# Two layers on one core: first expert's weights loaded beside the routing, a small sine network moved beside another layer's product, unused output tiles zeroed early

## The chip, the core and the metric

The kernel runs on one core of a Trainium2 chip. A core has five engines with a program each: TensorE (PE, matrix products), VectorE (DVE), ScalarE (ACT), GpSimd (POOL) and SyncE (SP), which here mostly issues DMA transfers. They share an on-chip memory of 128 partitions (SBUF), an accumulator memory (PSUM) and 16 DMA engines. The metric is the device time of one execution in microseconds (us), lower is better.

## The reference, cut to what matters

The program is two layers over 1024 rows of 1024 fp32 numbers. The first is a mixer (two recurrences), an output product with a residual and a norm, and a mixture of 32 experts of which each row takes two:

```python
def hier_moe(h, wg, bg, we, be, w_gate, w_up, w_down):
    """Top-1 expert group, then top-2 experts within it; gate = p(group) * softmax(top-2 logits)."""
    ...
    ids = (g_sel * EXPERTS_PER_GROUP + top_i).reshape(-1).astype(jnp.int32)
    order = jnp.argsort(ids)
    tok = order // TOP_K
    xs = xf[tok]
    sizes = jnp.bincount(ids, length=N_EXPERTS).astype(jnp.int32)
    hg = lax.ragged_dot(xs, w_gate.astype(xs.dtype), sizes)
    hu = lax.ragged_dot(xs, w_up.astype(xs.dtype), sizes)
    ys = lax.ragged_dot(jax.nn.silu(hg) * hu, w_down.astype(xs.dtype), sizes)
    ...
```

The second layer has a long convolution whose filters come from positions alone, by a small network of sines. It depends on weights and a table of positions, and on nothing that the first layer computes:

```python
    h = jnp.sin(sf[0] * (feats @ fw1.astype(f32) + fb1.astype(f32)))
    h = jnp.sin(sf[1] * (h @ fw2.astype(f32) + fb2.astype(f32)))
    h = jnp.sin(sf[2] * (h @ fw3.astype(f32) + fb3.astype(f32)))
    h = (h @ fw4.astype(f32)).reshape(L, HY_ORDER, 2, HY_WIDTH)
```

With this kernel's inputs (drawn from a fixed seed) the routing gives each of the 32 experts between 29 and 112 rows, counted with the reference's router on the host. So every expert fills one tile of 128 rows and none fills two.

## The kernel before, in words

The order of the work is written out by hand: the program is a sequence of stages (`Stage`), each with one instruction list per engine, semaphores between them, and a barrier of all five engines at its end (L118). What an engine does in a stage starts only when all engines have ended the stage before. Every fp32 operand of a large product is split in two: a rounded part "hi", which ACT copies, and the rest "lo", which DVE subtracts from the original. A product is then three matmuls (`products3`, L156 to L158).

The stages that the change touches, in the order in which they run, with P = 128 rows a tile:

- **g1** (`gemm`, 58 to 640 us) is the first layer's input product. While it runs, POOL sets 47 tiles of the DRAM array `xs` to zero from one zero row block in SBUF (`clear`, L401 to L407): the sorted rows of the experts are written into it later, and unused places must be zero.
- **go** (`deep_norm`, L3639, 948.4 to 1189.9 us) is the output product: 4 passes over 2 row tiles, 16 units of the contraction each, 64 units in all. A unit loads a 128x1024 block of weights (SP), ACT makes its hi (L3813), DVE its lo (L3882) and the lo of 256 columns of activations (L3887), TensorE does 12 matmuls. Weights and halves have three buffers. From the second pass on DVE and ACT also do residual and norm of the pass before.
- **route** (L1374, 1190 to 1258 us) picks the experts, counts, sorts, and leaves in `tile_exp` for each of 47 tiles the expert that it belongs to, and the number of tiles used (`n_used`). SP loads constants and the rows `h2t`; POOL scatters rows to `xs`.
- **moe** (`experts`, L1528 to L1731, 1258.9 to 1903.4 us) loops over the 47 tiles. For a tile SP loads its 128 rows of `xs` and three weight matrices of 2 MB, each in two halves of 1 MB (`weights`, L1572 to L1575), from the expert named in `tile_exp`; each load of a half waits until the lo of the tile before has been taken from that place. A DMA with a false condition (`cond`) moves nothing and counts its semaphore all the same. For the 15 tiles behind the last used one ACT runs `skipped` (L1693 to L1695): it stores whatever is in the buffer `y`, so that the DRAM array `ys` is written everywhere.
- **hf** (`hyena_spectrum`, L2012, 2434.1 to 2654 us) starts with the sine network: SP issues 18 small loads (L2053 to L2060), then the 1.8 MB table of transform matrices (L2061), the 1 MB `w4` in two halves (L2063), `skip` and the window (L2065). TensorE, DVE and ACT run the three layers of the network in a chain (L2104 to L2113, L2151 to L2166, L2133 to L2135), then TensorE multiplies with `w4` (`filters`) and DVE multiplies with the window (L2176). The table's lo is POOL's (L2148).
- **hc** (`hyena`, L2197) is the convolution itself. POOL makes the lo of its two tables, `ft_lo` and `it_lo` (L2347 to L2352).

## Time and profile before

| what | us |
|---|---|
| median of 3 runs | 4482.77 (4481.86 to 4484.9) |
| the profiled execution | 4481.31 |
| its span (first to last instruction) | 4479.5 |
| stage g1 | 58 to 640 |
| stage go | 948.4 to 1189.9 |
| stage route | 1190 to 1258 |
| stage moe | 1258.9 to 1903.4 |
| stage hf | 2434.1 to 2654 |

Over the span TensorE is busy for 3660.7 us (82%), DVE for 2936.8 us (66%), ACT for 1695.2 us (38%) and POOL for 66.7 us (1%). Since each stage ends in a barrier, the end of the program moves by what each stage gains or loses, and each stage has to be read for itself. A row of the timeline gives the start, the duration, the engine, the line and the operation with its shapes; in brackets stands how long the engine had been idle and what released it. SPq and ACTq are the DMA queues that SP and ACT issue to; their time is that of issuing, and the landing comes later.

### The profile page before, as it was taken

Reading aid. Unit: us, or ns where it says so; the run is one execution under the profiler, and the core shown is the slowest. Engines: PE = TensorE matmul, PEld = TensorE weight load, DVE = VectorE, ACT = ScalarE, POOL = GpSimd, SP = SyncE. Lnnn points to the kernel's source line nnn. Section 1 sums busy time; section 2 is a strip of 40 time slices with the busy share of each in tenths; the row PEclk is TensorE's granted clock in tenths of the full one; section 3 lists DMA queues with packets and bytes.
Section 4 is the critical chain, followed back from the end, with each engine's and each line's share of the span. In section 5 each row is a group of like instructions: output and inputs, shape, how many; then the busy total and the mean of one; then the engine's idle time right before and its main releaser. Section 6 shows DMA issues by size and latency. Waiting matters only on the chain. (4 is left out here: it accounts for less than half of the span.)

```text
span 4479.5 us, 63351 instructions
## 1 busy us (share of the span) xinstructions
PE 3660.7 (82%) x25152; PEld 2997.1 (67%) x25152; DVE 2936.8 (66%) x3525; ACT 1695.2 (38%) x2202; POOL 66.7 (1%) x49
## 2 busy tenths in 40 slices
PE   6999966879769999739997454546999786999898
PEld 4888856768657777628885243316998465888786
DVE  4774327966458888778874779884555546666455
ACT  3222113545257777633332132262333224323244
POOL 0000000000010000010000000000000000000000
PEclk8999988989779999859998576778999798999999
DMA  6523216646399999753332032263110332222465
GB/s 232 196 85 108 86 52 190 198 148 193 128 365 399 398 398 398 284 184 103 105 122 103 21 123 71 90 155 97 41 41 24 131 122 76 85 85 85 157 194 166
DMA packets 355480, 698.57 MB, mean 156 GB/s; under 512 B 55400, under 2 KB 159864, under 8 KB 353050
## 3 DMA queue, kind: packets, MB, share of 16 engines
q1 hardware_dynamic: 321754, 578.34, 37.8%
q10 hardware_dynamic: 22688, 74.98, 4.4%
q0 software_dynamic: 10784, 41.70, 2.4%
q8 instruction: 180, 2.95, 0.3%
q14 instruction: 74, 0.61, 0.0%
HBM read 535.88 MB, written 170.60 MB: 158 GB/s over the span
## 5 line engine op out<-in xcount | busy, mean ns | idle before, releaser
L1709 DVE TENSOR_TENSOR moe_wg_lo<-moe_wg,moe_wg_hi 128x2048 fp32r<-128x2048 f32 x68 | 155.6, 2291 | 69.5 <-ACT moe_wg_hi L1663 69.5
L156 PE MATMUL g_ps<-h1T_hi,g_w_lo 128*128 128x512 f32 x448 | 175.2, 391 | 7.0 <-DVE g_w_lo L339 7.0
L157 PE MATMUL g_ps<-h1T_lo,g_w_hi 128*128 128x512 f32 x448 | 175.0, 391 | 0.0
L158 PE MATMUL g_ps<-h1T_hi,g_w_hi 128*128 128x512 f32 x448 | 174.9, 390 | 0.0
L1663 ACT ACTIVATE moe_wg_hi<-moe_wg 128x2048 fp32r<-128x2048 f32 x68 | 130.2, 1918 | 95.0 <-DMA moe_wg<-in_exp_w_gate 95.0
L156 PE MATMUL g_ps<-x2T_hi,g_w_lo 128*128 128x512 f32 x352 | 140.0, 398 | 24.3 <-DVE g_w_lo L558 24.3
L3882 DVE TENSOR_TENSOR x3T_lo<-fd_w_raw,x3T_hi 128x1024 fp32r<-128x1024 f32 x66 | 80.8, 1224 | 120.1 <-ACT x3T_hi L3813 119.9
L2793 PE MATMUL rs_p_p<-rs_pm,rs_qx 64*64 64x64 f32 x2048 | 157.6, 217 | 0.0
L156 PE MATMUL fd_acc<-x3T_hi,x3T_lo 128*128 128x512 f32 x352 | 139.7, 397 | 18.3 <-DVE x3T_lo L3885 18.3
L1709 DVE TENSOR_TENSOR moe_wu_lo<-moe_wu,moe_wu_hi 128x2048 fp32r<-128x2048 f32 x68 | 152.5, 2282 | 1.8 <-ACT moe_wu_hi L1663 1.8
L156 PE MATMUL g_ps<-g_w_hi,h1T_lo 128*128 128x512 f32 x384 | 149.4, 389 | 0.0
L157 PE MATMUL g_ps<-g_w_lo,h1T_hi 128*128 128x512 f32 x384 | 149.4, 389 | 0.0
L158 PE MATMUL g_ps<-g_w_hi,h1T_hi 128*128 128x512 f32 x384 | 149.4, 389 | 0.0
L1709 DVE TENSOR_TENSOR moe_wd_lo<-moe_wd,moe_wd_hi 128x2048 fp32r<-128x2048 f32 x66 | 147.9, 2281 | 0.0
L2793 PEld LDWEIGHTS rs_p_p<-rs_pm,rs_qx 64*64 64x64 f32 x2048 | 143.8, 134 | 0.1
L157 PE MATMUL g_ps<-x2T_lo,g_w_hi 128*128 128x512 f32 x352 | 140.0, 398 | 0.0
L158 PE MATMUL g_ps<-x2T_hi,g_w_hi 128*128 128x512 f32 x352 | 139.5, 396 | 0.0
L1663 ACT ACTIVATE moe_wu_hi<-moe_wu 128x2048 fp32r<-128x2048 f32 x68 | 129.7, 1912 | 25.2 <-DMA moe_wu<-in_exp_w_up 25.2
L157 PE MATMUL fd_acc<-x3T_lo,x3T_hi 128*128 128x512 f32 x352 | 139.1, 395 | 0.0
L158 PE MATMUL fd_acc<-x3T_hi 128*128 128x512 f32 x352 | 138.9, 395 | 0.0
L1663 ACT ACTIVATE moe_wd_hi<-moe_wd 128x2048 fp32r<-128x2048 f32 x66 | 126.5, 1920 | 24.4 <-DMA moe_wd<-in_exp_w_down 24.3
L383 DVE COPY g_st<-g_ps 128x512 f32<-128x512 f32 x24 | 16.6, 691 | 177.5 <-PE g_ps L158 177.5
(702 smaller groups left out, 11000.3 us busy)
## 6 DMA issues: line engine op xcount, KB each, us to landing
moe_wg<-in_exp_w_gate SPq DMA_DIRECT2D x68, 1024.0 KB
moe_wu<-in_exp_w_up SPq DMA_DIRECT2D x68, 1024.0 KB
moe_wd<-in_exp_w_down SPq DMA_DIRECT2D x66, 1024.0 KB
fd_w_raw<-in_ffn_w_down SPq DMA_DIRECT2D x66, 512.0 KB, 4.4
go_w_raw<-in_w_out SPq DMA_DIRECT2D x64, 512.0 KB
...
s_xs<-g_zero POOLq DMA_DIRECT2D x1, 24064.0 KB, 82.8
...
```

Of the source, the lines that this page charges most:

```text
L156: pe.matmul(out, l[1], r[0], start=(k == 0), stop=False)
L157: pe.matmul(out, l[0], r[1], start=False, stop=False)
L158: return pe.matmul(out, l[0], r[0], start=False, stop=(k == kt - 1))
L383: v.tensor_copy(st[:, j % 2, 2 * i + 1], ps[:, 2 * i + 1]).then_inc(by_dve, 1)
L1663: act.activation(hi[:, q * m:q * m + m], w[:, q * m:q * m + m], ACT.Copy).then_inc(sem_hi, 1)
L1709: v.tensor_tensor(lo[:, q * m:q * m + m], w[:, q * m:q * m + m], hi[:, q * m:q * m + m], ALU.subtract).then_inc(sem_lo, 1)
L2793: mm = pe.matmul(p_p[g][o, p], q, pm[o, k], start=True, stop=True)
L3882: v.tensor_tensor(w_lo[:, n % NB], w_raw[:, n % NR], w_hi[:, n % NB], ALU.subtract).then_inc(w_low, 1)
```

## The change

**The experts' weights.** The three fp32 weight buffers now belong to the caller and live through route and moe. In route SP loads expert 0's gate, up and down weights (3 x 2 MB) right behind `h2t` and waits for them at its end. `tile_exp` has 48 more columns: for each tile whether its expert differs from that of the tile before (for the first tile: from expert 0), times `n_used`. In moe a weight load is made only if that value is over the tile's number; SP reads two more values a step for it.

**Unused tiles.** In g1 POOL clears, behind the 47 tiles of `xs`, also the last 31 tiles of `ys` (16.25 MB). In moe the 15 stores of `skipped` become a `nop` that counts the same semaphore.

**The sine network** is now a class `FilterNet` that runs as an `aside` in go, and stores its 128x512 result to DRAM (`net`); hf loads it with one transfer.

**POOL's subtractions** in hf (`tb_lo`) and hc (`ft_lo`, `it_lo`) are DVE's now. In hf the table's load stands behind those of h, w4 and skip.

```diff
@@ gemm
-                pool.dma_start(rows(clear)[:, 0:N_TILE], bc(zero[:, :].unsqueeze(1), [P, N_TILE, D])).then_inc(zeroed, 16)
-                pool.wait_ge(zeroed, 16)
+                for to in clear:
+                    n = to.shape[0] // P
+                    pool.dma_start(rows(to), bc(zero[:, :].unsqueeze(1), [P, n, D])).then_inc(zeroed, 16)
+                pool.wait_ge(zeroed, 16 * len(clear))
@@ route
             sp.dma_start(h2t[:, :, :], rows(h2)).then_inc(h_in, 16)
+            for dst, src in first:
+                sp.dma_start(dst[:, :, :], rows(src)).then_inc(w_in, 16)
+            sp.wait_ge(w_in, past(16 * len(first)))
...
+            v.tensor_scalar(te[:, N_LIST + 1:N_LIST + 2], te[:, 0:1], 0.0, None, ALU.not_equal)
+            v.tensor_tensor(te[:, N_LIST + 2:], te[:, 1:N_LIST], te[:, 0:N_LIST - 1], ALU.not_equal)
+            v.tensor_copy(tile_exp[:, N_LIST:N_LIST + 1], te[:, N_LIST:N_LIST + 1])
+            v.drain()
+            v.tensor_scalar(tile_exp[:, N_LIST + 1:], te[:, N_LIST + 1:], te[:, N_LIST:N_LIST + 1], None, ALU.mult)
@@ experts
+            def fresh(j):
+                return sp.value_load(tile_exp[0:1, bass.ds(j + (N_LIST + 1), 1)], min_val=0, max_val=N_TILE)
...
-            def weights(sem, w, src, e, j, n_used, q):
+            def weights(sem, w, src, e, j, limit, q):
                 n = w.shape[1] // 2
                 sp.dma_start(w[:, q * n:q * n + n], src.rearrange("e (q k p) n -> e q p k n", p=P, q=2)[e, q],
-                             cond=(n_used > j)).then_inc(sem[q], 16)
+                             cond=(limit > j)).then_inc(sem[q], 16)
...
             def skipped(j, b):
-                act.dma_start(ys.rearrange("(j p) n -> j p n", p=P)[j - 1], y[:, 1 - b]).then_inc(stored[1 - b], 16)
+                act.nop().then_inc(stored[1 - b], 16)
@@ hyena_spectrum
-            sp.dma_start(ft[:, :], feats_t).then_inc(got, 16)
-            sp.dma_start(wa[:, :], w1).then_inc(got, 16)
...
-            sp.dma_start(raw, table).then_inc(table_in, 16)
+            sp.dma_start(h[:, :], net).then_inc(got, 16)
             for r in half:
                 sp.dma_start(w4_raw[r], w4.rearrange("p (o d n) -> p o d n", o=2, d=2)).then_inc(got4, 16)
             sp.dma_start(sk[:, :, :], skip.rearrange("(a o) n -> a o n", a=1)).then_inc(got4, 16)
+            sp.dma_start(raw, table).then_inc(table_in, 16)
...
+            v.wait_ge(got4, past(48))
+            v.tensor_tensor(wp[:, :, 0], w4_raw[:, :, 0], w4_raw[:, :, 1], ALU.add)
+            v.tensor_tensor(wp[:, :, 1], w4_raw[:, :, 0], w4_raw[:, :, 1], ALU.subtract).then_inc(summed, 1)
+            v.wait_ge(tab_high, past(1))
+            v.tensor_tensor(tb_lo[:, :, :], raw, tb_hi[:, :, :], ALU.subtract).then_inc(tab_low, 1)
@@ hyena
-        @block.gpsimd
-        def _(pool):
-            pool.wait_ge(ft_high, past(1))
-            pool.tensor_tensor(ft_lo[:, :, :], raw, ft_hi[:, :, :], ALU.subtract).then_inc(ft_low, 1)
-            pool.wait_ge(it_high, past(1))
-            pool.tensor_tensor(it_lo[:, :, :], i_raw, it_hi[:, :, :], ALU.subtract).then_inc(it_low, 1)
...
+            v.wait_ge(ft_high, past(1))
+            v.tensor_tensor(ft_lo[:, :, :], raw, ft_hi[:, :, :], ALU.subtract).then_inc(ft_low, 1)
...
                     if i:
                         rest(i - 1)
+                    if c == 0 and i == 1:
+                        v.wait_ge(it_high, past(1))
+                        v.tensor_tensor(it_lo[:, :, :], i_raw, it_hi[:, :, :], ALU.subtract).then_inc(it_low, 1)
+class FilterNet:
...
+    def multiply(self, pe, q):
+        if q == 0:
+            pe.wait_ge(self.got, past(18 * 16))
+        else:
+            pe.wait_ge(self.sine, past(q))
+        for c, r in enumerate(self.HALF):
+            if q:
+                w = (self.wb, self.wc)[q - 1]
+                mm = pe.matmul(self.ps[r, :], w[r, :], self.h[r, :], start=True, stop=True)
+            else:
+                mm = pe.matmul(self.ps[r, :], self.wa[:, :], self.ft[:, c * 512:c * 512 + 512], start=True, stop=True)
+        mm.then_inc(self.product, 1)
+
+    def reduce(self, v, q):
+        k, m = self.k, self.m
+        v.wait_ge(self.got, past(18 * 16))
+        v.wait_ge(self.product, past(q + 1))
...
+    def activate(self, act, q):
+        act.wait_ge(self.arg, past(q + 1))
+        act.activation(self.h[:, :], self.m[:, :], ACT.Sin).then_inc(self.sine, 1)
+
+    def store(self, sp):
+        sp.wait_ge(self.sine, past(3))
+        sp.dma_start(self.out, self.h[:, :]).then_inc(self.kept, 16)
@@ deep_norm
+        ASIDE, AHEAD = (5, 15, 25), 4
...
+                if aside is not None and n == 2:
+                    aside.load(sp)
+                if aside is not None and n == ASIDE[2] + 3 * AHEAD:
+                    aside.store(sp)
...
+                if aside is not None and n in ASIDE:
+                    aside.multiply(pe, ASIDE.index(n))
...
                 split(n)
+                if aside is not None and n - AHEAD - 1 in ASIDE:
+                    aside.activate(act, ASIDE.index(n - AHEAD - 1))
...
                 split(n)
+                if aside is not None and n - AHEAD in ASIDE:
+                    aside.reduce(v, ASIDE.index(n - AHEAD))
```

So TensorE does a layer of the network behind units 5, 15 and 25 of go, DVE its eight instructions behind its part of units 9, 19 and 29, and ACT the sine behind its part of units 10, 20 and 30.

VectorE's instructions in the second pass of go, around units 19 and 20, before; `go_w_lo` and `go_a_lo` are the lo parts of a unit's weights and activations:

```order
L3882 TENSOR_TENSOR go_w_lo<-go_w_raw,go_w_hi 128x1024
L3887 SCALAR_TENSOR_TENSOR go_a_lo<-mixT,go_fac,go_a_hi 128x256
L3882 TENSOR_TENSOR go_w_lo<-go_w_raw,go_w_hi 128x1024
L3887 SCALAR_TENSOR_TENSOR go_a_lo<-mixT,go_fac,go_a_hi 128x256
L3905 TENSOR_SCALAR go_var<-go_ssq 128x1 x2
L3882 TENSOR_TENSOR go_w_lo<-go_w_raw,go_w_hi 128x1024
L3887 SCALAR_TENSOR_TENSOR go_a_lo<-mixT,go_fac,go_a_hi 128x256
```

And after, at the same place:

```order
L3943 TENSOR_TENSOR go_w_lo<-go_w_raw,go_w_hi 128x1024
L3948 SCALAR_TENSOR_TENSOR go_a_lo<-mixT,go_fac,go_a_hi 128x256
L3659 TENSOR_SCALAR go_net_m<-go_net_ps,go_net_bb,go_net_sf 128x512
L3661 TENSOR_SCALAR go_net_k<-go_net_m 128x512
L3663 TENSOR_SCALAR go_net_k<-go_net_k 128x512
L3665 TENSOR_SCALAR go_net_k<-go_net_k 128x512
L3668 SCALAR_TENSOR_TENSOR go_net_m<-go_net_k,go_net_m 128x512 x3
L3670 TENSOR_SCALAR go_net_m<-go_net_m 128x512
L3943 TENSOR_TENSOR go_w_lo<-go_w_raw,go_w_hi 128x1024
L3948 SCALAR_TENSOR_TENSOR go_a_lo<-mixT,go_fac,go_a_hi 128x256
L3966 TENSOR_SCALAR go_var<-go_ssq 128x1 x2
```

The network's eight instructions (`go_net_m`, `go_net_k`) now stand in a row between unit 19's and unit 20's subtractions.

VectorE at the head of hf before, from the first layer of the network on; `hf_wp` is the sum and the difference of w4's halves:

```order
L2155 TENSOR_SCALAR hf_m<-hf_p_f,hf_bb,hf_sf 128x512
L2157 TENSOR_SCALAR hf_k<-hf_m 128x512
L2159 TENSOR_SCALAR hf_k<-hf_k 128x512
L2161 TENSOR_SCALAR hf_k<-hf_k 128x512
L2164 SCALAR_TENSOR_TENSOR hf_m<-hf_k,hf_m 128x512 x3
L2166 TENSOR_SCALAR hf_m<-hf_m 128x512
L2169 TENSOR_TENSOR hf_wp<-hf_f 128x2x512
L2170 TENSOR_TENSOR hf_wp<-hf_f 128x2x512
L2155 TENSOR_SCALAR hf_m<-hf_p_f,hf_bb,hf_sf 128x512
```

And after:

```order
L2133 TENSOR_TENSOR hf_wp<-hf_f 128x2x512
L2134 TENSOR_TENSOR hf_wp<-hf_f 128x2x512
L2136 TENSOR_TENSOR hf_tb_lo<-hf_w,hf_tb_hi 128x3456
L2142 TENSOR_TENSOR hf_f<-hf_p_f,hf_win 128x1024 x4
L2146 TENSOR_TENSOR hf_f<-hf_f,hf_sk 1x512
```

The network is gone, the table's subtraction stands behind `hf_wp` and ahead of the four window products.

SyncE's loads at the head of go before:

```order
L3695 DMA go_fac<-in_mix_norm 128x16
L3721 DMA go_w_raw<-in_w_out 128x1024 x3
L3724 DMA go_wr<-in_norm_w 128x1024
L3721 DMA go_w_raw<-in_w_out 128x1024
L3701 DMA go_r<-in_x 128x1024
L3721 DMA go_w_raw<-in_w_out 128x1024
```

And after:

```order
L3746 DMA go_fac<-in_mix_norm 128x16
L3772 DMA go_w_raw<-in_w_out 128x1024 x3
L3775 DMA go_wr<-in_norm_w 128x1024
L3632 DMA go_net_ft<-in_c_feats 33x1024
L3633 DMA go_net_wa<-in_hy_filt_w_2 33x64
L3636 DMA go_net_wb<-in_hy_filt_w_2 64x64
L3636 DMA go_net_wc<-in_hy_filt_w_2 64x64
L3638 DMA go_net_bb<-in_hy_filt_b_2 64x1
L3639 DMA go_net_sf<-in_hy_sin_freq 64x1
```

The network's loads (18, of which the first six are shown) stand behind the first three weight blocks and the norm's weights, and ahead of unit 3's block.

## Rows read from the trace of the kernel before

**Rows 1.** Busy time by stretch (start:end, length): PE, PEld, DVE, ACT, POOL, clock, DMA share, GB/s.

```profile
100.00:120.00 20.00, 20.00 (x90) 16.58 (x89) 14.98 (x14) 3.52 (x5) 0.00 (x0) 1.00 1.03 417
1030.00:1060.00 30.00, 28.69 (x157) 24.44 (x156) 15.68 (x20) 13.60 (x18) 0.00 (x0) 0.97 0.56 181
1190.00:1260.00 70.00, 18.98 (x88) 18.85 (x88) 16.85 (x99) 1.61 (x3) 15.36 (x16) 0.50 0.46 182
1400.00:1500.00 100.00, 97.56 (x458) 79.63 (x457) 89.23 (x56) 74.62 (x55) 0.00 (x0) 1.00 1.04 398
2434.00:2460.00 26.00, 3.25 (x8) 0.58 (x8) 5.88 (x9) 5.00 (x3) 3.19 (x1) 0.50 0.59 179
```

**Rows 2.** Transfers by destination and source (part 6): count, KB each, us to landing.

```profile
moe_wd<-in_exp_w_down SPq DMA_DIRECT2D x66, 1024.0 KB
s_xs<-g_zero POOLq DMA_DIRECT2D x1, 24064.0 KB, 82.8
```

**Rows 3.** Timeline, start of the expert stage: start, us, engine, line, operation, [idle<-releaser].

```profile
1260.05 0.97 SPq L1574 DMA_DIRECT2D moe_wg<-in_exp_w_gate  x2
1267.27 1.91 ACT L1663 ACTIVATE moe_wg_hi<-moe_wg 128x2048 fp32r<-128x2048 f32 x1 [1.87 <-DMA moe_wg<-in_exp_w_gate]
1269.21 2.29 DVE L1709 TENSOR_TENSOR moe_wg_lo<-moe_wg,moe_wg_hi 128x2048 fp32r<-128x2048 f32 x1 [2.55 <-ACT moe_wg_hi L1663]
```

**Rows 4.** Timeline, end of the expert stage, ScalarE's and SyncE's queues.

```profile
1881.10 17.07 ACTq L1695 DMA_DIRECT2D s_ys<-moe_y  x15
1903.42 2.20 SPq L1779 DMA_DIRECT2D nf_hw<-in_hy_conv_w  x3
```

**Rows 5.** Tile moe_y after 1880 us: durations ns min/median/max, and its landings.

```profile
L1695 ACTq DMA_DIRECT2D s_ys<-moe_y x15: 343/657/1194, 1881.1 to 1897.2; - x15
DMA to landing us min/median/max: 2.7/5.6/5.9
```

**Rows 6.** Timeline, head of the spectrum stage hf, in order of time.

```profile
2434.06 0.37 SPq L2053 DMA_DIRECT2D hf_ft<-in_c_feats  x1
2445.02 0.59 SPq L2061 DMA_DIRECT2D hf_w<-in_c_hft  x1
2446.71 1.97 PE L2112 MATMUL hf_p_f<-hf_ft,hf_wa 33*64 33x512 f32 x4 [18.93 <-DMA hf_sf<-in_hy_sin_freq]
2453.64 3.08 ACT L2132 ACTIVATE hf_tb_hi<-hf_w 128x3456 fp32r<-128x3456 f32 x1 [24.05 <-DMA hf_w<-in_c_hft]
2456.74 1.28 ACT L2135 ACT_TABLE_LOAD   x1
2456.81 7.46 POOL L2148 TENSOR_TENSOR hf_tb_lo<-hf_w,hf_tb_hi 128x3456 fp32r<-128x3456 f32 x1 [515.93 <-ACT hf_tb_hi L2132]
2458.72 6.63 DVE L2169 TENSOR_TENSOR hf_wp<-hf_f 128x1024 f32<-128x1024 f32 x1 [4.43 <-DMA hf_sk<-in_hy_skip]
2466.41 0.80 DVE L2155 TENSOR_SCALAR hf_m<-hf_p_f,hf_bb,hf_sf 128x512 f32<-128x512 f32 x1
2471.09 0.43 DVE L2166 TENSOR_SCALAR hf_m<-hf_m 128x512 f32<-128x512 f32 x1
2492.52 1.22 DVE L2176 TENSOR_TENSOR hf_f<-hf_p_f,hf_win 128x1024 f32<-128x1024 f32 x1 [2.19 <-PE hf_p_f L2084]
```

**Rows 7.** Timeline, the output product go in its first pass.

```profile
983.82 1.23 DVE L3882 TENSOR_TENSOR go_w_lo<-go_w_raw,go_w_hi 128x1024 fp32r<-128x1024 f32 x1 [1.10 <-ACT go_w_hi L3813]
986.54 1.23 DVE L3882 TENSOR_TENSOR go_w_lo<-go_w_raw,go_w_hi 128x1024 fp32r<-128x1024 f32 x1 [1.10 <-ACT go_w_hi L3813]
993.60 1.06 ACT L3813 ACTIVATE go_w_hi<-go_w_raw 128x1024 fp32r<-128x1024 f32 x1 [1.26 <-PE go_acc L158]
```

**Rows 8.** Timeline, the convolution stage hc.

```profile
2678.85 4.48 DVE L1924 TENSOR_TENSOR hc_w<-shT 128x2048 f32<-128x2048 f32 x2
2720.09 6.70 DVE L2397 TENSOR_TENSOR hc_w<-hc_w 128x512 f32<-128x512 f32 x1
2726.29 0.79 PE L156 MATMUL hc_ps<-hc_hi,hc_it_lo 128*128 128x512 f32 x1 [11.03 <-POOL hc_it_lo L2352]
```

More of the change, by code:

```diff
@@ L2132, in _ @@
             act.activation(tb_hi[:, :, :], raw, ACT.Copy).then_inc(tab_high, 1)
-            for q in range(3):
-                act.wait_ge(arg, past(q + 1))
-                act.activation(h[:, :], m[:, :], ACT.Sin).then_inc(sine, 1)
             for n in range(5):
@@ L3737, in _ @@
                 store(t)
-            for b in range(n_r):
-                sp.wait_ge(stored[b], past(16 * len(range(b, NT, n_r))))
+            for b in range(n_out):
+                sp.wait_ge(stored[b], past(16 * len(range(b, NT, n_out))))
+            if aside is not None:
+                aside.finish(sp)
         @block.gpsimd
```

177 lines of the change are left out of this document (91 added, 86 removed).

## The prediction

> **What bounds the kernel now.** I looked for the stages that the change touches and read each by itself, since a barrier ends each and only a stage's own last chain counts.
>
> First the busy time by stretch [rows 1]. In the middle of the expert stage the 16 DMA engines are busy all the time (share 1.04, 398 GB/s) while DVE, the busiest other engine that prepares weights, works 89.23 of 100 us: that stage is bound by transfers. In the output product go (1030 to 1060) TensorE is busy 28.69 of 30 us at a granted clock of 0.97: bound by TensorE. In g1 (100 to 120) TensorE is busy 20.00 of 20 us although the zeroing of `xs` drives the DMA to 417 GB/s. In route (1190 to 1260) the DMA share is 0.46.
>
> Then the transfers [rows 2]: a half of a weight matrix is 1.049 MB (1024 KB), and 66 such loads of `wd` are 33 steps of two, 32 used tiles and one that loads nothing. A used tile moves 6 x 1.049 + 0.52 (rows in) + 0.52 (rows out) = 7.34 MB, 18.4 us at 398 GB/s; DVE's work would let it go in 0.892 x 18.4 = 16.4 us.
>
> Then the timeline where stages begin and end: the start of the expert stage [rows 3], its end [rows 4, 5], the head of hf [rows 6], the units of go [rows 7] and the places in hc where POOL was waited for [rows 8].
>
> **A, start of the expert stage: -7 us (bounds -2 to -10).** Of all weight loads in the stage only expert 0's six halves go, since the 32 tiles have 32 different experts; "none twice in a row" finds nothing to skip. The six halves are 6.29 MB, 15.8 us at the stage's rate. But the stream of loads now starts later. Before, the first half was issued at 1260.05 [rows 3] into idle queues. After, the first load of weights is tile 1's gate, which must wait until tile 0's first half has been split. ACT was free at 1267.27 - 1.87 = 1265.40 (it then has x's hi behind it), copies 1.91 us, DVE subtracts 2.29 us: the first issue is at 1269.6, so 9.6 us later. In that gap x of tile 1 passes (1.3 us that the stream saves), and I give back 0.5 us for smaller gaps behind it, since the next halves follow at DVE's pace of 2.29 us while one takes 1.049/0.398 = 2.63 us on the DMA. -15.8 + 9.6 - 1.3 + 0.5 = -7.0. At best two of the remaining latencies overlap more (-10); at worst the cold start of 7.2 us (1260.05 to 1267.27) comes again in full behind the first load and little but 2 us is left. The 6.29 MB need 16 us in route, whose DMA share is 0.46 over 70 us [rows 1] and whose h2t is ahead of them in the queue; they end some 35 us before the stage does. Route itself gets three small DVE instructions and a drain: +0.5 us. SP's two further reads a step stand ahead of loads that have some 10 us of queued transfers before them: 0.
>
> The Trainium skill ("DMA: Bandwidth & Descriptors", section "Anatomy of one DMA — SWDGE (gpsimd) path") gives a transfer a fixed cost of about 2 us beside its bytes at about 436 GB/s, which is 4.4 us for 1 MB. The row shows 7.2 us for the cold start here, on another kind of queue, and the row decides; by the page the stream would be restarted sooner and A would be an estimated -9.
>
> **B, end of the expert stage: -15 us (-12 to -17).** The 15 stores of unused tiles hold ACT's queue for 17.07 us from 1881.10 [rows 4], the last lands 5.6 us (median) after issue [rows 5], and the next stage's first instruction is at 1903.42. The issues take 15 x 0.657 = 9.9 us, so each turn of the loop costs another (17.07 - 9.9)/14 = 0.5 us. After, 15 turns with a nop: 1880.8 + 15 x 0.5 = 1888.4. What is late next lies below it: the last real store, issued just before 1881, lands by 1886, and DVE's last subtraction ends at about 1884. Gain 1903.4 - 1888.4 = 15. A turn may cost 0.35 to 0.7 us, hence the bounds. The 16.25 MB are now written in g1, behind `xs`. There TensorE stayed at 20.00 of 20 under 417 GB/s [rows 1], `xs` took 82.8 us for 24 MB [rows 2], so `ys` ends some 56 us later, near 200, in a stage that ends at 640: 0. If its cover were gone it would cost up to its 56 us.
>
> **C, head of hf: -29 us (-27 to -34).** Before: 18 issues of 0.6 us from 2434.06 to 2445.02, then the table, which lands 8.6 us later at 2453.64; ACT's copy of it (3.08 us) stands ahead of the first sine, then come two more layers, and the fourth window product ends at 2492.52 + 1.22 = 2493.7 [rows 6]. After: the table is issued behind h, w4 and skip, at about 2436. The queue had both behind one another before: w4 and skip landed at 2458.72, 5.1 us after the table. So the sum of both is what the table now waits: 2434.06 + 0.3 + 8.6 + 5.1 + 0.6 (h, 0.26 MB) = 2448.6. ACT's copy to 2451.7. DVE now does the table's lo: 2.29 us for 2048 columns [rows 3] is 1.12 ns a column, 3456 columns are 3.87 us, to 2455.6. DVE did `hf_wp` before that, and the two PSUM buffers of the first window products are full. Two window products (1.22 each), then TensorE's third and fourth group at 3.41 us each (2.19 + 1.22 between windows), and the last window: 2455.6 + 1.2 + 3.4 + 3.4 + 1.2 = 2464.8. Gain 2493.7 - 2464.8 = 28.9. If the table lands without the 5.1 us, up to 5 us more; if h's transfer adds its own latency, 2 us less. DVE's `hf_wp` of 6.63 us shrinks, since POOL worked beside it (its 7.46 us instruction spans it), but it is off the last chain.
>
> **D, the network in go: +8 us (+4 to +16).** TensorE sets the end here and a unit takes 986.54 - 983.82 = 2.72 us [rows 7]. Per layer TensorE does two fp32 products, 1.97 us in hf [rows 6] at a clock of 0.50 [rows 1] and about 1.0 at 0.97. DVE gets a block of 2471.09 + 0.43 - 2466.41 = 5.1 us between two units' subtractions. It idles 1.10 us in each unit [rows 7], and its lo is up to one unit (2.7 us) ahead of TensorE thanks to three buffers: 5.1 - 1.1 - 2.7 = 1.3, with the smaller idle time in the passes that also do the norm 1.5 us of stall. Three times 1.0 + 1.5 is 7.5, and 0.5 for ACT, which does a table load of 1.28 us for the sine, another back to its root, and the sine of 0.63, and which idles 1.26 us a unit [rows 7]. If DVE's lead covers it all: 3 x 1.0 + 1 = 4. If ACT's six table loads all show: 7.5 + 6 x 1.28 = 15.2, say 16. SP's 18 issues (11 us) fall ahead of unit 3's load, where three units are in flight; up to 1.6 us late at the start of the stage, in the range.
>
> **E, hc: 0 (-3 to +4).** `ft_lo` (3200 columns x 1.12 = 3.6 us) goes ahead of DVE's first work at 2678.85. `it_lo` costs another 3.6 and about 1.5 of waiting, but a product of 6.70 us at 2720.09, beside POOL, becomes as short as others of 128x512 (0.80 us at 2466.41 [rows 6]), and TensorE, which waited 11.03 us for POOL's `it_lo` until 2726.29, is released some 3.4 us sooner [rows 8]: +3.6 - 3.4.
>
> **The sum.** -7 + 0.5 - 15 - 29 + 8 + 0 = -42.5, against the profiled execution of 4481.3: 4438.8. The median of the runs is 1.5 us above the profiled one: 4440.
>
> **Rivals.**
>
> *The network is dear in go.* If the table loads and the DVE block both show, D is +16 to +20 and the time some 4450. For: ACT's table load of 1.28 us is in the row, and with a norm in the same pass each sine costs two. Against: at 2456.74 the load is followed by the sine at once (2458.04), and ACT has slack. The Trainium skill ("ScalarE: Activation LUTs", section "What ACT_TABLE_LOAD costs") gives a switch about 2.66 us with its drain, twice the row; six of them would be 16 us and D at most an estimated +16 to +20 too. Chance 12%.
>
> *The start of the expert stage is worth something else.* All 15.8 us if the stream finds its pace at once (4431), or 2 us if a full cold start comes again (4445). Each for half of 6%.
>
> *The routing repeats experts*, so that the rule of the change bites: each repeat would drop up to 6.29 MB, but not below DVE's 16.4 us for 18.4: 2 us for most tiles, more where buffers run ahead; for all 31 it would be 62 us, about 4380. Against: the 32 experts have one tile each. 3%. This is also the case in which the change does more than its loads suggest; in the forecast that part does nothing.
>
> *Slower: TensorE's clock falls in go.* Each aside makes TensorE wait; if the granted clock falls to 1.2 GHz, a unit's matmuls (28.69/30 of 2.72 = 2.6 us at 0.97) take 2.6 x 0.97/0.50 = 5.05 us, so +2.3 a unit. Eighteen units at that clock eat the whole gain, and all of the 54 units behind the first aside would give +125 and 4565. Against: the clock was 0.97 there with DVE's and ACT's waits of 1.3 us in each unit. For: at the head of hf, where TensorE is busy 3.25 of 26 us, and in route it was 0.50 [rows 1]. 4%.
>
> **How the numbers follow.** The forecast has 75%: 4440. The range takes in the bounds of A to E that do not all fall to one side and the first two rivals: 4426 to 4458. A difference under 0.2% (9 us) can hardly be told from none in this kernel. The forecast, the third rival and most of the first two are faster by over 9 us: 0.94; the far end of the first is within 0.2%: 0.02; the last is slower: 0.04.
>
> **What the changed profile would show.** Route ends no later than before but for 0.5 us, and the first tile's hi starts at once. The first gate load of moe is issued near 9 us after the stage's start and the stage is 22 us shorter. ACT's nops end 7 to 8 us after the last real store. hf's fourth window product ends 31 us after its start instead of 60. go is 8 us longer, with three waits of TensorE near units 9, 19, 29, each of 1 to 2 us. It is wrong if go grows by over 16 us or its clock falls, if tiles in moe take another time than 18.4 us, or if g1 ends later.

## The result, and the profile after

The changed kernel takes 4439.24 us (median of 4 runs, 4436.19 to 4441.13) against 4483.36 us of the kernel before measured beside it (4 runs, 4481.86 to 4484.9): a ratio of 0.9898, 95% interval 0.9885 to 0.991. The forecast was 4440. The profiled execution took 4440.7 us, its span is 4438.9.

Since every stage ends in a barrier, the two traces can be set against each other stage by stage. This table is worked out from the times at which SyncE leaves the barriers. The stages that no edit touches differ here by -1.2 to +0.7 us, and by up to 2.8 us in single stages of the kernels further down, which is how far one profiled execution can be trusted.

| stage | before, us | after - before | forecast |
|---|---|---|---|
| g1 | 586.1 | +0.1 | 0 |
| go | 241.7 | +9.6 | +8 |
| route | 68.0 | +0.4 | +0.5 |
| moe | 645.3 | -20.9 | -22 |
| hf | 220.3 | -30.5 | -29 |
| hc | 243.2 | -0.1 | 0 |
| all | 4479.5 | -40.6 | -42.5 |

Start of moe, timeline of the changed kernel, all engines; it answers to [rows 3]:

```profile
1268.68 0.34 SPq L1611 DMA_DIRECT2D moe_x<-s_xs  x1
1274.79 3.70 ACT L1676 ACTIVATE moe_wg_hi<-exp_g 128x2048 fp32r<-128x2048 f32 x2
1276.72 4.49 DVE L1722 TENSOR_TENSOR moe_wg_lo<-exp_g,moe_wg_hi 128x2048 fp32r<-128x2048 f32 x2 [0.57 <-ACT moe_wg_hi L1676]
1279.33 2.53 SPq L1587 DMA_DIRECT2D exp_g<-in_exp_w_gate  x2
```

The stage begins at 1267.8. ACT splits gate weights at 1274.79 without a wait, and SyncE's first load that moves weights (tile 1's) is issued at 1279.33, once VectorE has taken the first half: 11.5 us after the stage's start, against 2.0 before. The forecast was 9.6 us of delay, and it is 9.5.

End of moe, and the tile moe_y behind 1880 us; they answer to [rows 4, 5]:

```profile
1883.02 4.49 DVE L1722 TENSOR_TENSOR moe_wd_lo<-exp_d,moe_wd_hi 128x2048 fp32r<-128x2048 f32 x2
1883.21 0.34 ACTq L1704 DMA_DIRECT2D s_ys<-moe_y  x1
1892.31 2.26 SPq L1792 DMA_DIRECT2D nf_hw<-in_hy_conv_w  x3
DMA to landing us min/median/max: 2.6/2.6/2.6
```

From the last real store to the next stage it is 9.1 us instead of 23.4. Busy time by stretch, columns as in [rows 1]:

```profile
160.00:200.00 40.00, 40.00 (x178) 33.12 (x177) 27.41 (x26) 9.65 (x12) 0.00 (x0) 1.00 0.96 380
1400.00:1500.00 100.00, 98.85 (x464) 81.23 (x463) 89.45 (x57) 76.14 (x55) 0.00 (x0) 1.00 1.04 399
```

The zeroing of ys runs in g1 at 160 to 200 (380 GB/s, 106 in the kernel before), and TensorE is busy for 40.00 of 40 us. In the middle of moe nothing has changed: 399 GB/s, DMA share 1.04.

Head of hf, timeline; it answers to [rows 6]:

```profile
2423.25 0.34 SPq L2058 DMA_DIRECT2D hf_h<-s_net  x1
2425.35 0.37 SPq L2062 DMA_DIRECT2D hf_w<-in_c_hft  x1
2431.85 1.23 DVE L2133 TENSOR_TENSOR hf_wp<-hf_f 128x1024 f32<-128x1024 f32 x1 [14.16 <-DMA hf_sk<-in_hy_skip]
2435.97 3.08 ACT L2120 ACTIVATE hf_tb_hi<-hf_w 128x3456 fp32r<-128x3456 f32 x1 [17.19 <-DMA hf_w<-in_c_hft]
2439.09 3.76 DVE L2136 TENSOR_TENSOR hf_tb_lo<-hf_w,hf_tb_hi 128x3456 fp32r<-128x3456 f32 x1 [4.88 <-ACT hf_tb_hi L2120]
2442.76 2.35 DVE L2142 TENSOR_TENSOR hf_f<-hf_p_f,hf_win 128x1024 f32<-128x1024 f32 x2
2451.26 1.22 DVE L2142 TENSOR_TENSOR hf_f<-hf_p_f,hf_win 128x1024 f32<-128x1024 f32 x1 [2.19 <-PE hf_p_f L2082]
```

The table lands 12.7 us after the stage's start and the fourth window product ends at 2452.48, 29.2 us after it, instead of 59.7.

The first layer of the network in go, VectorE, ScalarE and one wait of TensorE; it answers to [rows 7]:

```profile
986.23 1.23 DVE L3943 TENSOR_TENSOR go_w_lo<-go_w_raw,go_w_hi 128x1024 fp32r<-128x1024 f32 x1 [1.17 <-ACT go_w_hi L3872]
987.77 0.80 DVE L3659 TENSOR_SCALAR go_net_m<-go_net_ps,go_net_bb,go_net_sf 128x512 f32<-128x512 f32 x1
989.34 1.28 ACT L3675 ACT_TABLE_LOAD   x1
992.47 0.43 DVE L3670 TENSOR_SCALAR go_net_m<-go_net_m 128x512 f32<-128x512 f32 x1
992.93 0.63 ACT L3675 ACTIVATE go_net_h<-go_net_m 128x512 f32<-128x512 f32 x1 [2.31 <-DVE go_net_m L3670]
993.04 1.23 DVE L3943 TENSOR_TENSOR go_w_lo<-go_w_raw,go_w_hi 128x1024 fp32r<-128x1024 f32 x1
994.81 0.47 PE L156 MATMUL go_acc<-go_w_hi,go_a_lo 128*128 128x512 f32 x1 [1.55 <-DVE go_a_lo L3948]
997.82 1.06 ACT L3872 ACTIVATE go_w_hi<-go_w_raw 128x1024 fp32r<-128x1024 f32 x1 [1.57 <-PE go_acc L158]
```

The network's eight instructions stand from 987.77 to 992.9, unit 10's subtraction comes behind them without idle time, and TensorE waits 1.55 us for VectorE (994.81). ACT's next copies run on until TensorE is the one waited for again (997.82).

hc, VectorE's timeline and TensorE's waits (us in total, times, longest); it answers to [rows 8]:

```profile
2637.21 3.48 DVE L2320 TENSOR_TENSOR hc_ft_lo<-hc_w,hc_ft_hi 128x3200 fp32r<-128x3200 f32 x1
2681.11 3.49 DVE L2364 TENSOR_TENSOR hc_it_lo<-hc_w,hc_it_hi 128x3200 fp32r<-128x3200 f32 x1 [1.42 <-ACT hc_it_hi L2307]
PE hc_ps L156 <- DVE hc_it_lo L2364: 7.3, 1, 7.3
```

TensorE waits 7.3 us for `it_lo` where it waited 11.0, and `ft_lo` takes 3.5 us ahead of VectorE's work on `hc_w`.

### The profile page after: what moved, and what is told of

Same layout as the page of the kernel before. It is cut to its first block and busy times, and to the rows that moved or that the text cites. A ratio compares the mean times of both kernels' runs of the same rounds, so it can differ in the third digit from the quotient of the medians.

```text
span 4438.9 us, 63596 instructions
## 1 busy us (share of the span) xinstructions
PE 3662.6 (83%) x25152; PEld 2998.5 (68%) x25152; DVE 2935.5 (66%) x3531; ACT 1694.4 (38%) x2203; POOL 46.9 (1%) x47
## 5 line engine op out<-in xcount | busy, mean ns | idle before, releaser
L1722 DVE TENSOR_TENSOR moe_wg_lo<-exp_g,moe_wg_hi 128x2048 fp32r<-128x2048 f32 x68 | 155.1, 2291 | 61.8 <-ACT moe_wg_hi L1676 61.8
L1676 ACT ACTIVATE moe_wg_hi<-exp_g 128x2048 fp32r<-128x2048 f32 x68 | 129.5, 1917 | 74.5 <-DMA exp_g<-in_exp_w_gate 74.5
L156 PE MATMUL fd_acc<-x3T_hi,x3T_lo 128*128 128x512 f32 x352 | 139.4, 396 | 19.7 <-DVE x3T_lo L3946 19.6
L1722 DVE TENSOR_TENSOR moe_wu_lo<-exp_u,moe_wu_hi 128x2048 fp32r<-128x2048 f32 x68 | 152.5, 2283 | 2.7 <-ACT moe_wu_hi L1676 2.7
L1722 DVE TENSOR_TENSOR moe_wd_lo<-exp_d,moe_wd_hi 128x2048 fp32r<-128x2048 f32 x66 | 148.0, 2282 | 0.2
L1676 ACT ACTIVATE moe_wu_hi<-exp_u 128x2048 fp32r<-128x2048 f32 x68 | 129.0, 1911 | 18.7 <-DMA exp_u<-in_exp_w_up 18.7
L1676 ACT ACTIVATE moe_wd_hi<-exp_d 128x2048 fp32r<-128x2048 f32 x66 | 125.7, 1916 | 19.2 <-DMA exp_d<-in_exp_w_down 19.2
```

What stands on the lines that cost most here:

```text
L156: pe.matmul(out, l[1], r[0], start=(k == 0), stop=False)
L1676: act.activation(hi[:, q * m:q * m + m], w[:, q * m:q * m + m], ACT.Copy).then_inc(sem_hi, 1)
L1722: v.tensor_tensor(lo[:, q * m:q * m + m], w[:, q * m:q * m + m], hi[:, q * m:q * m + m], ALU.subtract).then_inc(sem_lo, 1)
```

## Experiments

Three kernels have one part of the change each; others change one thing in the changed kernel or try to better it. The edits are shown in part. Stage times are those of each one's profiled execution, times are medians; the kernel before measured beside them took 4483.4, 4484.5 and 4485.6 us in the three groups.

### One part alone

**a1_end**: the kernel before with the early zeroing and the nop.

```diff
-                act.dma_start(ys.rearrange("(j p) n -> j p n", p=P)[j - 1], y[:, 1 - b]).then_inc(stored[1 - b], 16)
+                act.nop().then_inc(stored[1 - b], 16)
```

> The kernel before with one part of the change: the 31 last tiles of ys zeroed in g1 and a nop in place of the 15 stores. Theory (the two profiles: from the last real store's issue to the stage's end 23.4 us before, 9.0 us after): the stage moe is 14 to 15 us shorter than before, g1 within 0.3 us, total about 4469. Rival (the gain at the end needs the early loads too, or the zeroing costs g1): moe shorter by under 12 us or g1 longer by over 1 us, total above 4472.

4468.65 us, ratio 0.9964 (0.995 to 0.9979). moe is 15.5 us shorter, g1 0.2 longer, route 0.6 shorter. The theory holds: this part works without the rest, and the zeroing is hidden. Its end is even 1.1 us better than in the changed kernel: from the last real store to the end of the stage it is 7.9 us here and 9.0 there. In both VectorE comes to the barrier last, by its empty turns behind the last used tile. This is its loop's branch, one for two turns:

```profile
L1563 DVEq COMPARE_BRANCH  x8: 59/66/72, 1881.0 to 1886.8; - x8
```

That is 5.8 us for 14 turns, 0.41 us each; in the changed kernel a turn takes 0.49 (see b6_pairs). Why it takes longer when both changes of moe are in is open; in a2_first it takes 0.41 too.

**a2_first**: the kernel before with expert 0's weights loaded in route and the condition on repeats.

```diff
             sp.dma_start(h2t[:, :, :], rows(h2)).then_inc(h_in, 16)
+            for dst, src in first:
+                sp.dma_start(dst[:, :, :], rows(src)).then_inc(w_in, 16)
+            sp.wait_ge(w_in, past(16 * len(first)))
```

> The kernel before with one part of the change: expert 0's weights loaded in route, and the condition on weight loads. Theory (A of the prediction, as the profile after bears it out): moe 6.5 us shorter than before, route 0.4 us longer, total about 4477. Rival (the whole 15.8 us of the six halves, of which the end of the stage hides a part in the profile after): moe 12 to 16 us shorter, total about 4470.

4478.74 us, ratio 0.9988 (0.9979 to 0.9998). moe is 7.2 us shorter, route 1.2 longer. Not 15.8: the rival falls. (The 1.2 us of route say little: route is 0.6 us shorter in a1_end, which leaves it alone.) Where the gain sits shows in the distance between ScalarE's stores of a tile. Before, it is 18.45 us from the first tile on. Here the first store comes 3.3 us sooner, then four tiles take 17.7 us each and the fifth 18.2, and from there it is 18.4 as before.

**a3_net**: the kernel before with the network in go and hf's new loads, all three subtractions still on POOL.

```diff
                 if k < KT - 1:
                     mm.then_inc(used, 1)
+                if aside is not None and n in ASIDE:
+                    aside.multiply(pe, ASIDE.index(n))
```

> The kernel before with one part of the change: the sine network in go and the loads of hf in the new order, while POOL keeps its three subtractions. Theory: go 9.6 us longer, as in the profile after, and hf shorter by 27 to 32 us, since the window products do not need the table's lo and the removal of the network is what counts: total about 4463. Rival (DVE's subtraction of the table is what makes hf short): hf shorter by under 24 us, total above 4467.

4457.79 us, ratio 0.9941 (0.9924 to 0.9957). go +9.8, hf -31.3, hc +0.7. So the removal of the network, with the loads in their new order, makes hf short, not VectorE's subtraction. By the medians the three parts gain 14.8, 4.7 and 25.6 us, 45 in all, against 44.1 of the changed kernel: they add up.

**b1_pool**: the changed kernel with the three subtractions back on POOL.

```diff
+        @block.gpsimd
+        def _(pool):
+            pool.wait_ge(tab_high, past(1))
+            pool.tensor_tensor(tb_lo[:, :, :], raw, tb_hi[:, :, :], ALU.subtract).then_inc(tab_low, 1)
```

> The changed kernel with the subtractions of the tables in hf and hc back on POOL. Theory (E of the prediction and a window chain that then no longer waits for the table's lo): hc within 1 us, hf within 3 us of the changed kernel, total 4436 to 4443. Rival (DVE's share is worth its own): hf or hc longer by 4 to 8 us, total 4444 to 4450, as POOL's subtraction of 7.5 us takes twice DVE's 3.8 us and slows DVE's tensor_tensor beside it.

4436.33 us (4432.0 to 4441.97), which the changed kernel's 4439.24 (4436.19 to 4441.13) overlaps. hf is 0.8 us shorter than after, hc 0.9 longer: the move from POOL to VectorE is worth nothing in the two stages together, as E said of hc. In hf POOL's subtraction stands beside VectorE's window products:

```profile
2435.07 7.48 POOL L2133 TENSOR_TENSOR hf_tb_lo<-hf_w,hf_tb_hi 128x3456 fp32r<-128x3456 f32 x1 [509.49 <-ACT hf_tb_hi L2120]
2436.78 2.36 DVE L2145 TENSOR_TENSOR hf_f<-hf_p_f,hf_win 128x1024 f32<-128x1024 f32 x2 [6.96 <-DMA hf_win<-in_c_window]
```

Two of them take 2.36 us, as long as with POOL idle (b5_hf below), while in the kernel before `hf_wp` took 6.63 us beside the same subtraction and ended 1.1 us behind it [rows 6]. `hf_wp` has both its operands in SBUF, a window product has one in PSUM; that this is what decides is a guess, since no run changes it alone.

What caught the eye is go, where this kernel has the same instructions as the changed one: 248.6 us against 251.3. The last unit of go on TensorE, changed kernel:

```profile
1173.85 0.39 PE L158 MATMUL go_acc<-go_w_hi,go_a_hi 128*128 128x512 f32 x1
1174.36 0.63 PE L157 MATMUL go_acc<-go_w_lo,go_a_hi 128*128 128x512 f32 x1
1177.34 0.54 PE L158 MATMUL go_acc<-go_w_hi,go_a_hi 128*128 128x512 f32 x1
```

And the same unit in b1_pool:

```profile
1172.44 0.39 PE L156 MATMUL go_acc<-go_w_hi,go_a_lo 128*128 128x512 f32 x1
1174.25 0.39 PE L158 MATMUL go_acc<-go_w_hi,go_a_hi 128*128 128x512 f32 x1
```

And the granted clock (column after the engines) in the stretch of 4 us at that place in each, the changed kernel's first:

```profile
1174.00:1178.00 4.00, 3.88 (x11) 2.54 (x9) 1.23 (x2) 1.15 (x2) 0.00 (x0) 0.57 0.11 43
1171.00:1175.00 4.00, 3.64 (x20) 2.82 (x19) 1.47 (x2) 0.35 (x1) 0.00 (x0) 1.00 0.00 0
```

In the changed kernel a matmul takes 0.63 us instead of 0.39 from the fifth of the unit's twelve on, at a clock that has fallen to half: the unit costs 1.6 us more. The first transpositions behind it cost another 0.8 (1.97 us instead of 1.18), at a second fall that begins at 1181.0. Nothing waited ahead of the first fall: the row ahead is work of TensorE itself (the router's products of 36 columns). The kernel before and b1_pool pass the same place at full clock.

In the kernels whose layers stand where the changed kernel has them, or that have no network in go, a fall in the middle of go lasts 3.4 us and begins from 0.4 us before to 1.0 us behind the end of a run of router products, nearly always a pass's second (there are three such places in go). But not each place has one in each execution: the kernel before has two, b1_pool two, the changed kernel three, b4_copy two and b5_hf one. A fall costs TensorE about 1.7 us, and the one at the end 2.4 with the transpositions. What decides whether it comes is open.

Five kernels have the same instructions in go: the changed one, b1_pool, b5_hf, b6_pairs and d1_repeat. The stage is 9.6, 6.9, 7.4, 7.5 and 10.5 us longer in them than before.

### What the network costs in go

I followed the start of VectorE's weight subtraction in each of the 64 units against the kernel before, from the start of the stage. Each column is the delay in us; the last row is that of the whole stage, so it adds what happens behind unit 63.

| unit | after | b1_pool | b3_spread | b4_copy | b2_loads | b7_go |
|---|---|---|---|---|---|---|
| 0 | +2.6 | +1.7 | +1.8 | +1.8 | +0.1 | +0.3 |
| 5 | +1.4 | +1.0 | +1.0 | +1.0 | +0.1 | +0.3 |
| 12 | +4.4 | +4.0 | +2.4 | +3.9 | +0.1 | +0.3 |
| 18 | +4.4 | +4.1 | +2.3 | +4.0 | +0.1 | +2.9 |
| 22 | +7.6 | +7.2 | +3.3 | +5.9 | +0.2 | +4.5 |
| 28 | +6.9 | +6.7 | +3.5 | +5.8 | +6.5 | +6.7 |
| 33 | +7.2 | +6.9 | +3.5 | +6.2 | +9.9 | +11.2 |
| 48 | +7.2 | +6.9 | +3.5 | +4.5 | +18.6 | +10.0 |
| 63 | +7.3 | +7.0 | +3.6 | +4.6 | +17.1 | +8.5 |
| stage | +9.6 | +6.9 | +3.5 | +6.9 | +17.8 | +10.8 |

**b2_loads**: the network's loads late and in pairs, its layers behind units 23, 33 and 43.

```diff
-        ASIDE, AHEAD = (5, 15, 25), 4
+        ASIDE, AHEAD = (23, 33, 43), 4
-                if aside is not None and n == 2:
-                    aside.load(sp)
+                if aside is not None and 11 <= n < 20:
+                    aside.load(sp, n - 11)
```

> The changed kernel, the network's 18 loads issued two at a time behind SP's loads of units 11 to 19 of go, and its three layers moved from behind units 5, 15, 25 to behind units 23, 33, 43. Theory (the profile after: the first ACT copy of go waits 2.4 us longer for the router's weights, which POOL's queue loads beside the 18 small ones, and 1.4 us of it reach TensorE): unit 4's subtraction is back within 0.3 us of its place before, go is 1.4 us shorter than after, but for the 2.3 to 2.7 us that a fall of the clock inside the last unit costs or does not. Rival (SP's 11 us of issuing ahead of unit 3's load delay the stage): then the first hi is still late by 2.4 us. Rival (the delay is a matter of chance): unit 4 stays 1.4 us late.

4448.34 us. The start is back in its place (+0.1): the theory on it holds. It holds in all 13 other profiles: without the early loads the start is at most 0.3 us late, with them 1.0 to 3.3 us (unit 5). What ScalarE's first copy waits for, in the kernel before, the changed one and this one (us in total, times, longest):

```profile
ACT go_f_hi L3851 <- DMA router_w<-in_router_e_w: 9.6, 1, 9.6
ACT go_f_hi L3910 <- DMA router_w<-in_router_e_w: 12.2, 1, 12.2
ACT go_f_hi L3911 <- DMA router_w<-in_router_e_w: 9.7, 1, 9.7
```

The router's weights come by POOL's queue, and with 18 small loads on SyncE's this copy starts 2.6 us later (12.2 - 9.6; in the eight profiles with the early loads it is 1.7 to 3.0). But go as a whole became 8.2 us longer than after, which I had not expected: by units 33, 42 and 50 the three layers have cost 9.8, 4.1 and 3.1 us, in passes in which VectorE also does residual, norm and router work. The clock falls to half five times instead of three, once for 6.8 us, and twice where TensorE had waited for VectorE and done no router products.

**b3_spread**: VectorE's eight instructions of a layer over five units.

```diff
+                for q, at in enumerate(ASIDE if aside is not None else ()):
+                    if 0 <= n - at - AHEAD < 5:
+                        aside.reduce(v, q, n - at - AHEAD)
```

> The changed kernel, DVE's eight instructions of a layer spread over five units (one or two behind each unit's own), the sine one unit later than the last of them. Theory (D of the prediction: the block of 5.1 us is longer than DVE's lead): the stalls of about 1.8 us behind units 9 and 19 go, and go is 3 to 4 us shorter than after at the same state of the clock in the last unit (5.6 to 6.6 us over before instead of 9.6). Rival (what costs is TensorE's own two products and their place): go stays within 1 us.

go is +3.5 us instead of +9.6. Of the 6.1 us 2.3 are the clock at the end and 0.4 the start, neither of them the edit's; 3.4 are the two stalls, and neither wait of TensorE (1.55 and 1.50 us in the changed kernel) is in this trace. VectorE's timeline at the place shown above:

```profile
987.81 0.81 DVE L3660 TENSOR_SCALAR go_net_m<-go_net_ps,go_net_bb,go_net_sf 128x512 f32<-128x512 f32 x1
988.99 1.23 DVE L3947 TENSOR_TENSOR go_w_lo<-go_w_raw,go_w_hi 128x1024 fp32r<-128x1024 f32 x1 [0.37 <-ACT go_w_hi L3876]
990.52 0.42 DVE L3662 TENSOR_SCALAR go_net_k<-go_net_m 128x512 f32<-128x512 f32 x1
991.02 0.43 DVE L3664 TENSOR_SCALAR go_net_k<-go_net_k 128x512 f32<-128x512 f32 x1
991.71 1.23 DVE L3947 TENSOR_TENSOR go_w_lo<-go_w_raw,go_w_hi 128x1024 fp32r<-128x1024 f32 x1 [0.26 <-ACT go_w_hi L3876]
993.25 0.42 DVE L3666 TENSOR_SCALAR go_net_k<-go_net_k 128x512 f32<-128x512 f32 x1
993.75 0.69 DVE L3668 SCALAR_TENSOR_TENSOR go_net_m<-go_net_k,go_net_m 128x512 f32<-128x512 f32 x1
994.51 1.23 DVE L3947 TENSOR_TENSOR go_w_lo<-go_w_raw,go_w_hi 128x1024 fp32r<-128x1024 f32 x1
```

The subtractions of units 10 to 12 stay 2.7 us apart. In total the kernel takes 4438.4 us (4431.92 to 4440.37), which the runs can't tell from the changed kernel's.

**b4_copy**: a copy in place of the sine, so that ACT's tables stay; the network is not computed.

```diff
-        act.activation(self.h[:, :], self.m[:, :], ACT.Sin).then_inc(self.sine, 1)
+        act.activation(self.h[:, :], self.m[:, :], ACT.Copy).then_inc(self.sine, 1)
```

> The changed kernel, ACT's sine of the network replaced by a copy, so that no table load stands in go for it (h is not the network's then, and the output is another). Theory: ACT's slack hides both table loads, go is within 0.5 us of the changed kernel at the same state of the clock in the last unit, total within 3 us. Rival (first rival of the prediction: table loads on the path): go shorter by 4 to 8 us.

4436.51 us (4435.85 to 4439.47). go is 2.7 us shorter than after, though it has the late fall of the clock too. Of that 1.8 us come between units 33 and 34, where this execution lacks one of the falls that the kernel before has. Against b1_pool, which starts alike, 0.7 to 1.3 us are left, and they come behind the second layer (5.9 against 7.2 at unit 22), where ACT has the table load back to the root in the chain. So the first rival had a grain of truth, an eighth or so of what it needed.

### hf, and the end of moe

**b5_hf**: the table's subtraction behind the second window product.

```diff
-            v.wait_ge(tab_high, past(1))
-            v.tensor_tensor(tb_lo[:, :, :], raw, tb_hi[:, :, :], ALU.subtract).then_inc(tab_low, 1)
+                    if n == 0 and c == 1:
+                        v.wait_ge(tab_high, past(1))
+                        v.tensor_tensor(tb_lo[:, :, :], raw, tb_hi[:, :, :], ALU.subtract).then_inc(tab_low, 1)
```

> The changed kernel, DVE's subtraction of the table in hf behind the second window product instead of ahead of the first. Theory (C of the prediction: the window products wait for the table's lo only because it stands ahead of them in DVE's list): the first window product starts 2 to 5 us sooner, TensorE's third and fourth group run beside the subtraction, hf is 2.5 to 4.5 us shorter than after. Rival (the window itself lands no sooner, or the first transform waits for the table's lo): hf within 1 us.

4435.62 us (4431.99 to 4443.3), hf 0.6 us shorter than after. The theory's 2.5 us were wrong, and its rival (the window lands no sooner) has it. VectorE's timeline:

```profile
2438.82 2.36 DVE L2140 TENSOR_TENSOR hf_f<-hf_p_f,hf_win 128x1024 f32<-128x1024 f32 x2 [6.99 <-DMA hf_win<-in_c_window]
2441.09 3.75 DVE L2144 TENSOR_TENSOR hf_tb_lo<-hf_w,hf_tb_hi 128x3456 fp32r<-128x3456 f32 x1
2444.76 1.22 DVE L2140 TENSOR_TENSOR hf_f<-hf_p_f,hf_win 128x1024 f32<-128x1024 f32 x1
2447.33 1.22 DVE L2140 TENSOR_TENSOR hf_f<-hf_p_f,hf_win 128x1024 f32<-128x1024 f32 x1 [1.35 <-PE hf_p_f L2082]
```

The window's transfer, last in SyncE's queue, lands 17.9 us after the stage's start. In the changed kernel, with the subtraction ahead, the first window product starts at 19.6 us, so 1.7 us was all that could be had. The window products end 27.6 us after the start instead of 29.2, and a part of the 1.6 is lost again behind them. The 0.6 us are small but likely real: hf is 31.1 to 31.7 us shorter than before in the four kernels where VectorE has no subtraction ahead of the window products (a3_net, b1_pool, b5_hf, c1_all), and 29.5 to 30.8 in the seven others that have moved the network.

**b6_pairs**: SyncE, TensorE and VectorE pass two unused tiles with one branch.

```diff
+                    with eng.If(n_used >= i * 2 + first):
+                        body(i * 2 + first, b0, i + first // 2, n_used)
+                        run(i * 2 + (first + 1), 1 - b0, i + (first + 1) // 2)
```

> The changed kernel; in moe the loops of SP, TensorE and DVE over the tiles test two steps with one branch where both are unused (ACT, which has its nops, keeps its loop). Theory (profile after: ACT is through with its nops 6.5 us after the last real store, DVE with its own empty turns 2.2 us later, and the stage ends there): moe is 1.5 to 2.5 us shorter than after. Rival (B of the prediction as worked out: ACT's nops end the stage): moe within 0.5 us of after.

4435.03 us (4432.08 to 4438.46). From the last store to the end it is 7.2 us instead of 9.0, as the theory had it. In all the stage is 3.5 us shorter, but the other 1.6 us come at its start, where six tiles instead of four take 17.7 us, and most of that is not the edit's: in the kernels whose moe is the changed kernel's the last store falls between 614.1 (b4_copy) and 615.4 us of the stage, here at 613.8. The loop's branch in the changed kernel, behind the last used tile:

```profile
L1570 ACTq COMPARE_BRANCH  x8: 48/53/53, 1883.8 to 1889.5; - x8
L1570 DVEq COMPARE_BRANCH  x8: 59/66/72, 1884.9 to 1891.7; - x8
```

For 14 turns ACT needs 5.7 us (0.41 each) and VectorE 6.8 (0.49 each), and VectorE is through 2.2 us later. So ACT's nops (through 6.5 us after the last store) did not end the stage in the changed kernel: VectorE's own empty turns did.

### The rival on repeats

**d1_repeat**: every second tile gets the expert of the one before it, so half of the experts' weights are not used.

```diff
+            v.tensor_copy(te[:, 1:N_LIST:2], te[:, 0:N_LIST - 1:2])
```

> The changed kernel, in which every second tile is given the expert of the tile before it, so that 16 of the 32 used tiles find their weights loaded and skip six halves of 1 MB each (the output is not the reference's: half of the experts' weights are not used). Theory (DMA sets a tile's 18.4 us, DVE's work its floor of 16.4): a pair takes 32.8 us of DVE instead of 36.8, 4 us a pair, moe 50 to 64 us shorter than after. Rival (loads are the whole cost): 16 x 15.8 = 253 us shorter. Rival (the condition does not bite, or the engines' waits for one another are the pace): within 20 us of after.

4427.74 us, ratio 0.9868 (0.9851 to 0.9884). moe is 16.7 us shorter than after, 1.0 us for each of 16 repeats; but all tiles are faster, those with new weights too. The theory and the first rival missed; the third has the number, and what sets the pace is this. Busy time in the middle of the stage:

```profile
1400.00:1500.00 100.00, 100.00 (x474) 83.15 (x473) 93.02 (x58) 76.95 (x58) 0.00 (x0) 1.00 0.64 230
```

The transfers fall to 230 GB/s, so the condition bites. VectorE is at 93.02, and TensorE at 100.00 of 100: each tile takes 17.7 us, and that is TensorE's floor, only 0.7 below the DMA's 18.4. I had taken VectorE's 16.4 for the next limit, though the same row of the kernel before had TensorE at 97.56.

### Put together

**b7_go**: loads three at a time behind units 3 to 8, layers behind units 9, 19, 29, VectorE's instructions spread. **c1_all**: b7_go, b6_pairs and b5_hf in one.

```diff
-        ASIDE, AHEAD = (5, 15, 25), 4
+        ASIDE, AHEAD = (9, 19, 29), 4
-                if aside is not None and n == 2:
-                    aside.load(sp)
+                if aside is not None and 3 <= n < 9:
+                    aside.load(sp, n - 3)
```

> The changed kernel, the network's loads three at a time behind SP's loads of units 3 to 8 of go, its layers behind units 9, 19, 29, and DVE's eight instructions of a layer spread over five units. Theory (start 1.4 us and stalls of 3.7 us are what the profiles of b2_loads and b3_spread take out): go 1 to 3.5 us over before instead of 9.6, but for 2.3 us at its end and 1.7 us each for falls of the clock. Rival (later layers cost more wherever they are, as in b2_loads): go 6 us or more over before.

> b7_go, b6_pairs and b5_hf in one kernel. Theory: their gains add, go 6 to 8 us shorter than after, moe 2, hf 0.6: total 4427 to 4432. Rival (they do not add, or the clock takes them back): above 4435.

b7_go takes 4443.6 us (4439.7 to 4444.1), go +10.8. The start costs 0.3 and the first layer 1.2, as hoped, but moving the others from 15 and 25 to 19 and 29 costs what the spread had saved. Behind unit 15 a pass ends and TensorE waits for VectorE anyway: 1.3 us in the kernel before, 0.3 in the changed one, so the second layer there fills a wait. In b7_go that wait is 2.7 us, a later one 2.6 us, and within or at the end of each the clock falls to half for 3.4 us, as in c1_all at the same places and in no kernel with layers at 5, 15 and 25. The rival was right. c1_all takes 4436.66 us (4436.24 to 4438.96): moe -24.2 and hf -31.7 add up as expected, go (+10.7) takes it back. None of these beats the changed kernel by more than the runs can tell. The kernel that the profiles point to, b3_spread's places with b6_pairs, was not run; what is the edits' own in them, 3.4 us of stalls and 1.8 at the end of moe, makes an estimated 5 us.

## Why the prediction was right

**A, start of moe: right in sum, a piece of the way to it not seen.** The delay of the first load was 9.5 us for 9.6, and the stage to the last real store is 6.5 us shorter for 7.0 (6.5 to 7.9 in the eight profiles with this part and no other edit in moe, 7.2 in the mean). But the 15.8 us do not simply come off a stream: the first tile gains 2.6 us and four tiles run at TensorE's 17.7 us before the stream limits again. That is one of the prediction's own signs of being wrong (tiles that take another time than 18.4 us), and that the sum came out so close without it is in part luck. By the Trainium skill's fixed cost of about 2 us ("DMA: Bandwidth & Descriptors", section "Anatomy of one DMA — SWDGE (gpsimd) path") A would have been an estimated -9; the measured 6.5 to 7.9 us stand nearer to the sum by the row, but with the first tiles bound by TensorE they do not test the page's cost.

**B, end of moe: 14.3 us for 15, one step wrong.** A turn of ACT with a nop takes 0.41 us for 0.5, so ACT is through 6.5 us after the last store and not 7 to 8; the last store lands at 1886. The step "DVE's last subtraction ends at about 1884" was right for its place (4.3 us behind the last store). What it left out are VectorE's own empty turns, which end 2.2 us later than ACT. b6_pairs shows it. The two misses, one each way, nearly cancel.

**C, head of hf: 30.5 us for 29.** The table landed 12.7 us after the start for 14.5, the later steps came as worked out, and `hf_wp` shrank to 1.23 us. That the window lands last of all was not seen; it would have capped a larger gain (b5_hf).

**D, go: 9.6 us for 8, its terms mis-sized against each other.** One layer was priced at 1.0 + 1.5. The first two cost 3.0 and 2.8 us (units 5 to 12 and 18 to 33): TensorE's products 1.1, and a wait behind VectorE's block of 1.55 and 1.50 (b3_spread takes away both). The third cost nothing, and the third of the three waits forecast near units 9, 19 and 29 did not come; it lies near a pass's end, but no run moves it alone, so that this is the reason is only argued. 1.4 us at the start came from the router's weights, a transfer of another queue, and not from unit 3's load as I had it. 2.4 us at the end came from the granted clock. So 8 and 9.6 are near each other in part by luck: 2.5 us too much for the third layer stand against 3.8 that the sum did not have.

The ACT tables were 0.7 to 1.3 us of their allowance of up to 8. The allowance counted six loads, two for each sine; the trace has four (at 989.34, 1025.50, 1052.98 and 1079.5), since the second sine finds its table still in place. The second of them:

```profile
1025.50 1.28 ACT L3898 ACT_TABLE_LOAD   x1
1026.79 0.29 ACT L3898 ACTIVATE go_root<-go_var 128x1 f32<-128x1 f32 x2
```

The Trainium skill's 2.66 us a switch ("ScalarE: Activation LUTs", section "What ACT_TABLE_LOAD costs") would be an estimated 11 us for the four. The part for the drain is not seen at 1025.50, where the load takes 1.28 us and the next instruction starts at once.

**E, hc, g1 and route: as worked out.** -0.1, +0.1 and +0.4, all within what one execution differs from another.

**The rivals.** The clock's rival was the right place with the wrong size: the granted clock did fall in go, but for single stretches of 3.4 us, and that also in the kernel before. The 0.97 of [rows 1] is such a fall and no steady clock: it is 1.00 from 1030 to 1058 and 0.51 from 1058.4 to 1061.9. Of repeats there are none in this routing, and 16 of them were worth 1 us each, not 2. The second rival's 15.8 us were seen in no run.
